# Layer norm's root on four columns, the third modulation product summed by VectorE, and vectors turned first

## What is computed

```python
sc_l = jax.nn.silu(c)
mod_l = (sc_l @ w_mod[i] + b_mod[i])[:, None, :]
sh1_l, s1_l, g1_l, sh2_l, s2_l, g2_l = jnp.split(mod_l, 6, axis=-1)
hl = modulate(rms_norm(xl, norm1_g[i]), sh1_l, s1_l)
...
u = h @ w_pw1 + b_pw1
a, gate = jnp.split(u, 2, axis=-1)
u = a * jax.nn.sigmoid(gate)
u = dwconv(...) + b_dw
u = jax.nn.silu(layer_norm(u, ln_g, ln_b))
yl = u @ w_pw2 + b_pw2
...
xl = xl + g1_l * yl
xl = xl + g2_l * sq_relu_mlp(modulate(rms_norm(xl, norm2_g[i]), sh2_l, s2_l), mlp_w1[i], mlp_w2[i])
```

## Time and profile before

| what | value |
|---|---|
| median of 3 runs | 2220.65 us (2217.94, 2220.65, 2222.88) |
| span of the profiled execution | 2221.3 us, its own time, 0.65 above that median |
| PE busy | 2162.8 us (97%) |
| DVE busy | 989.9 us (45%) |
| ACT busy | 374.7 us (17%) |
| POOL busy | 75.3 us (3%) |
| chain that ended last | PE 66%, issue 23%, DMA 6%, DVE 4%, ACT 1% |
| HBM read | 561.05 MB, 254 GB/s over the span |

### The profile page before, as it was taken

One profiled execution on the slowest core, in us unless ns is written; L12 is line 12 of the kernel. 1 busy time (PEld: TensorE's weight loads), 2 busy tenths in 40 slices (PEclk: granted clock), 3 DMA queues, 4 the chain that ended last, 5 costly groups with the idle time before them and its releaser, 6 DMA issues.

```text
span 2221.3 us, 25048 instructions
## 1 busy us (share of the span) xinstructions
PE 2162.8 (97%) x10192; PEld 1318.6 (59%) x10192; DVE 989.9 (45%) x1433; ACT 374.7 (17%) x743; POOL 75.3 (3%) x94
## 2 busy tenths in 40 slices
PE   7999999999999999998999999999999899999999
PEld 3443588888886777855444444437888544444443
DVE  2983397798845534833112222215555322222222
ACT  3013312012123112842100000002000200000000
POOL 1110100000021000000000000001000000000000
PEclk9999999999999999997999999999999899999999
DMA  9538244677541112032899999996112499999997
GB/s 349 189 95 296 76 152 152 238 259 282 206 171 38 39 52 77 1 152 114 356 429 428 429 428 429 428 424 254 60 76 91 205 422 429 429 428 428 429 428 301
DMA packets 110139, 570.26 MB, mean 257 GB/s; under 512 B 9929, under 2 KB 18670, under 8 KB 82414
## 3 DMA queue, kind: packets, MB, share of 16 engines
q1 hardware_dynamic: 107328, 564.55, 63.3%
q10 hardware_dynamic: 2734, 4.64, 0.9%
HBM read 561.05 MB, written 2.10 MB: 254 GB/s over the span
## 4 chain that ended last, share of the span: by engine, by line
PE 66%; issue 23%; DMA 6%; DVE 4%; ACT 1%; ACTq 0%; POOL 0%; SPq 0%; DVEq 0%; POOLq 0%
PE psum L1677 22%; PE psum L2142 9%; PE psum L1417 6%; PE psum L2126 4%; PE psum L1825 4%; PE psum L1849 3%; DMA ring<-in_moe_w_down_dram 3%; PE psum L2006 2%; PE psum L2234 2%; PE psum L2180 2%; DMA ring<-in_mlp_w_dram 2%; PE psum L1982 2%; PE psum L1957 2%; PE psum L1624 1%; DVE arena L2475 1%
## 5 line engine op out<-in xcount | busy, mean ns | idle before, releaser
L2142 PE MATMUL psum<-ring,arena 128*64 128x512 f32 x2048 | 445.0, 593 | 4.3 <-DMA ring<-in_moe_w_up_dram 4.3
L2142 PEld LDWEIGHTS psum<-ring,arena 128*64 128x64 f32 x2048 | 144.9, 137 | 299.0 <-issue 286.5
L2126 PE MATMUL psum<-ring,arena 128*64 128x512 f32 x768 | 224.5, 594 | 2.0 <-DMA ring<-in_moe_w_down_dram 2.0
L3036 DVE TENSOR_TENSOR arena<-psum,arena 128x512 f32<-128x512 f32 x32 | 33.9, 1059 | 384.9 <-PE psum L2142 384.9
L1417 PE MATMUL psum<-hT,ring 128*128 128x512 f32 x416 | 182.9, 600 | 3.0 <-ACT hT L938 3.0
L1677 PE MATMUL psum<-ring 128*128 128x256 f32 x640 | 142.9, 380 | 2.2 <-DVE roots L2619 2.2
L1417 PEld LDWEIGHTS psum<-hT,ring 128*128 128x128 f32 x416 | 79.6, 192 | 103.6 <-issue 98.6
L1677 PE MATMUL psum<-hT,ring 128*128 128x256 f32 x608 | 139.5, 386 | 0.8 <-ACT hT L932 0.8
L1677 PEld LDWEIGHTS psum<-ring 128*128 128x128 f32 x640 | 121.0, 190 | 22.1 <-issue 5.9
L2180 PEld LDWEIGHTS psum<-arena 128*128 128x128 f32 x1024 | 121.2, 198 | 14.0 <-issue 14.0
L1677 PEld LDWEIGHTS psum<-hT,ring 128*128 128x128 f32 x608 | 117.6, 194 | 18.7 <-issue 2.2
(11 more groups left out here) (417 smaller groups left out, 2535.8 us busy)
## 6 DMA issues: line engine op xcount, KB each, us to landing
ring<-in_moe_w_gate_dram SPq DMA_DIRECT2D x64, 2048.0 KB, 19.1
ring<-in_moe_w_up_dram SPq DMA_DIRECT2D x64, 2048.0 KB, 16.2
ring<-in_moe_w_down_dram SPq DMA_DIRECT2D x44, 2048.0 KB, 19.7
ring<-in_ada_w_dram SPq DMA_DIRECT2D x24, 2048.0 KB, 8.7
ring<-in_mlp_w_dram SPq DMA_DIRECT2D x16, 2048.0 KB, 8.6
hT<-in_moe_w_down_dram SPq DMA_DIRECT2D x16, 2048.0 KB, 14.6
ring<-in_w_mod_dram SPq DMA_DIRECT2D x12, 2048.0 KB, 13.6
ring<-in_conv_w_in_dram SPq DMA_DIRECT2D x6, 2048.0 KB, 19.4
```

The source lines that it names most:

```text
L2126: ins = pe.matmul(psum[64 * e:64 * e + 64, bank + nh, :], src[:, 4 * h + k, 64 * e:64 * e + 64], w[:, k, nh * N:(nh + 1) * N], start=h == ...
L2142: ins = pe.matmul(psum[64 * nh:64 * nh + 64, bank + e, :], src[:, 4 * h + k, 64 * e:64 * e + 64], w[:, k, nh * N:(nh + 1) * N], start=h == ...
```

## The change

**Start.** T_V is turned ahead of `norm_stat(NORM1)`. ACT begins with a one-element SiLU, takes SiLU of c before the root, and so loads its table before the first squares. The first block of `pw1` lands on two semaphores, one for each half.

**Layer norm.** `norm_stat(LN)` becomes eight `token_sums`; the root and reciprocal are taken on 128x4 values; `token_widen(LN)` spreads them into a bank that DVE's `scale` reads directly. A one-element square root goes ahead of the squares.

**Round 2.** `mod_gemv(2)` leaves PE. DVE multiplies and accumulates the four blocks with eight instructions of 2048 columns (`mod_rows_of`), PE sums the result over partitions with four matmuls (`mod_sum(2)`) ahead of tile 5 of `pw2`, and `mod_turn(2)` stands ahead of tile 6. POOL does NORM2's sums before round 2's bias. Weights of the MLP's first two blocks now wait for DVE's reading of round 2.

**Widening.** All widening is done by `pe.transpose` where it was a matmul.

```diff
@@ constants, stream
+MOD_SUMS = {2: (2, 0), 3: (3, 1), ...}
+MOD2_ORDER = (2, 3, 0, 1)
-                    ("mod_row", rnd + 1)) for b in range(4)]
+                    ("mod_part", MOD2_ORDER.index(b) + 1) if rnd == 2 else ("mod_row", rnd + 1)) for b in range(4)]
@@ ACT
             act.wait_ge(S["pads_zero"], 5)
+            act.activation(tok[:, 2, 0:1], one[:, 0:1], ACT.Silu)
             squares(NORM1, xT, emptied(T_X))
-            root(NORM1)
             act.wait_ge(*emptied(T_V)(0))
             act.activation(cpad[:, :, 0:3], ..., ACT.Silu).then_inc(S["c_silu"], 1)
+            root(NORM1)
...
+            act.activation(tok[:, 2, 0:1], one[:, 0:1], ACT.Sqrt)
             squares(LN, cv, lambda j: (S["centered"], j + 1))
-            root(LN)
+            token_root(LN)
             shift(LN, hT, vecT[:, COL["ln_b"]:COL["ln_b"] + 8], ACT.Silu)
-            mod_row(2)
-            mod_turned(2)
...
+                if j == 4:
+                    mod_row(2)
+                if j == 5:
+                    mod_turned(2)
@@ PE
-                    ins = pe.matmul(psum[...], n_tok[:, 1, tt:tt + 1].to_broadcast([P, P]), ident,
-                                    start=True, stop=True, skip_group_check=True)
+                    ins = pe.transpose(psum[...], n_tok[:, 1, tt:tt + 1].to_broadcast([P, P]), ident)
...
-            norm_stat(NORM1)
             pe.wait_ge(S["vec_in"], 16 * N_VEC)
             turn_tile(T_V, ...)
+            norm_stat(NORM1)
...
-            norm_stat(LN)
-            mod_gemv(2)
             for j in range(DT):
-                if j == 1:
+                pe.wait_ge(S["sq_ready"], DT * LN + j + 1)
+                token_sums(sq[:, j % 2, :], j == 0, j == DT - 1).then_inc(S["sq_used"], 1)
+            token_widen(LN)
+            for j in range(DT):
+                if j == 5:
+                    mod_sum(2)
+                if j == 6:
                     mod_turn(2)
@@ DVE
+            def mod_rows_of(b):
+                acc = carve(arena, 10240, 4 * N)
+                w = arrived(dve, B_MOD[2][b])
+                for k in range(2):
+                    c = cpad[:, 2 * b + k, 0:1]
+                    ... ins = tensor_scalar or scalar_tensor_tensor(out=acc, in0=w[:, k, :], scalar=c, in1=acc, ...)
+            for b in MOD2_ORDER[0:2]:
+                mod_rows_of(b)
             for j in range(DT):
+                if j in (1, 2):
+                    mod_rows_of(MOD2_ORDER[j + 1])
                 dve.wait_ge(FREE["act"], tile_free[T_PW2 + j][1])
                 dve.tensor_tensor(xT[:, j, :], xT[:, j, :], tmp[:, j % 2, :], ALU.add).then_inc(S["x_pw2"], 1)
```

More of the change, by code:

```diff
@@ L246, in block_kernel @@
             loads[2] -= PAIRS
-        loads[slot] += len(src) if isinstance(src, list) else 1
+        loads[slot] += len(src) if isinstance(src, list) and n != B_PW1[0] else 1
         landed_at.append((slot, 16 * loads[slot]))
@@ L543, in block_kernel @@
         IN_HALVES = {NORM2: 0, MIX1: 1}
+        INVERSES = {LN: 1, NORM2: 2, MIX1: 3}
         HALF_ORDER = [(j, half) for js, half in ((0, 0), (0, 1), (4, 1), (4, 0)) for j in range(js, js + 4)]
@@ L564, in load @@
                     for m, dst in enumerate(slot_like(slot, src)):
-                        sp.dma_start(dst, src[m]).then_inc(landed[slot], 16)
+                        sp.dma_start(dst, src[m]).then_inc(S["pw1_first"] if (n, m) == (B_PW1[0], 0) else landed[slot], 16)
                 else:
@@ L814, in _ @@
                 .then_inc(S["gains"], 1)
+            sum_squares(NORM2)
+            mod_bias(2)
             make_gain(1, 0, 32, ("norm2_g", 0))
-            sum_squares(NORM2)
             for rnd in range(3, 9):
@@ L918, in token_root @@
             def token_root(n):
-                if n == NORM2:
-                    act.wait_ge(S["sq_used"], DT * NORM2 + DT)
+                if n == MIX1:
+                    act.wait_ge(S["n_ms"], 1)
                 else:
-                    act.wait_ge(S["n_ms"], 1)
+                    act.wait_ge(S["sq_used"], DT * n + DT)
                 act.activation(n_tok[:, 0, :], psum[:, STAT, 0:NT], ACT.Sqrt, bias=eps[:, 0:1])\
@@ L941, in mod_row @@
                 act.wait_ge(S["mod_row"], s + 1)
-                act.activation(mod_rows[:, :], psum[:, MISC, :], ACT.Copy, scale=1.0 if s < 3 else float(P))\
+                act.activation(mod_rows[:, :], psum[:, MISC, :], ACT.Copy, scale=1.0 if s < 2 else float(P))\
                     .then_inc(S["mod_row_sb"], 1)
@@ L1468, in token_widen @@
             def token_widen(n):
-                pe.wait_ge(S["n_inv"], IN_HALVES[n] + 1)
+                pe.wait_ge(S["n_inv"], INVERSES[n])
                 for tt in range(NT):
-                    ins = pe.matmul(psum[:, (MISC, STAT)[tt // 2], tt * P:(tt + 1) * P],
-                                    n_tok[:, 1, tt:tt + 1].to_broadcast([P, P]), ident,
-                                    start=True, stop=True, skip_group_check=True)
-                    if tt % 2:
+                    ins = pe.transpose(psum[:, STAT if n == LN else (MISC, STAT)[tt // 2], tt * P:(tt + 1) * P],
+                                       n_tok[:, 1, tt:tt + 1].to_broadcast([P, P]), ident)
+                    if tt == NT - 1 or tt % 2 and n != LN:
                         ins.then_inc(S["n_wide"], 1)
@@ L1541, in x_widen @@
                 for tt in range(NT):
-                    ins = pe.matmul(psum[:, bank, tt * P:(tt + 1) * P], x_inv[:, which, tt:tt + 1].to_broadcast([P, P]), ident,
-                                    start=True, stop=True, skip_group_check=True)
+                    ins = pe.transpose(psum[:, bank, tt * P:(tt + 1) * P], x_inv[:, which, tt:tt + 1].to_broadcast([P, P]), ident)
                 ins.then_inc(S["x_wide"], 1)
@@ L2369, in scale @@
             def scale(n, src, dst, gains, width=N, made=0):
-                if n:
-                    dve.wait_ge(S["scaled"], DT * SCALES[n])
-                dve.wait_ge(S["rms_ready"], n + 1)
-                link(dve.reciprocal(rstd[:, 0:width], rms[:, 0:width]))
+                if n == LN:
+                    dve.wait_ge(S["n_wide"], 1)
+                    inverse = psum[:, STAT, :]
+                else:
+                    dve.wait_ge(S["rms_ready"], n + 1)
+                    link(dve.reciprocal(rstd[:, 0:width], rms[:, 0:width]))
+                    inverse = rstd[:, 0:width]
                 if made:
@@ L2390, in scale_halves @@
                     j, half = HALF_ORDER[at]
-                    dve.wait_ge(S["n_wide"], 2 * IN_HALVES[n] + half + 1)
+                    dve.wait_ge(S["n_wide"], 2 * IN_HALVES[n] + half + 2)
                     dve.scalar_tensor_tensor(out=hT[:, j, H * half:H * half + H], in0=xT[:, j, H * half:H * half + H],
```

32 lines of the change are left out of this document (22 added, 10 removed).

## The result

| | before | after |
|---|---|---|
| median of 20 runs each, us | 2218.73 | 2223.17 |
| ratio after to before | | 1.0017, 95% interval 1.0011 to 1.0023 |
| span of the profiled execution, us | 2221.3 | 2222.2 |
| PE, DVE, ACT busy, us | 2162.8, 989.9, 374.7 | 2157.0, 1004.9, 373.2 |

By the ratio the change costs 3.8 us (2.4 to 5.1; the medians differ by 4.4), which is inside the 0.2% that was named as the bound of "no change". (One of the 20 executions after took 4566.84 us; the ratio leaves it out.) The forecast was 2223.3 us.

A forecast was written before the change was run, and what follows sets the result against it. PE, busy for 97% of the span, was taken to bound the kernel. Terms -1.4 + 2.8 + 2.2 + 0.9 - 1.8 = +2.7 us on the median 2220.65 gave 2223.3 us; range 2216.0 to 2227.0, the forecast's own 2220.3 to 2226.0.

The forecast's parts named there:

- step 1: Program's start: vectors turned before the norm's sums, SiLU before the root; round 0 begins at 25.0, not 26.41: -1.4 us.
- fourth rival: Program's start: vectors land 2 us later than in the one profile, so no gain there; +4.1, 2224.8 us; 8%.
- Step 2: Layer norm's root: one-column sums mostly at the lower clock, so `pw2` starts at 208.7, not 205.89: +2.8 us.
- first rival: Layer norm: the clock holds through the one-column sums and `pw2` loses nothing; -5.0, 2215.7 us; 12%.
- Step 3: Start of `pw2`: 4.4 us run at half speed because the clock is still low: +2.2 us.
- Step 4: Round 2: PE gets four 512-column matmuls back, DVE's eight added instructions stay hidden: +0.9 us.
- Step 5: Widening by transposes at NORM2, MIX1 and the mixer: four tiles cost 0.9, not 1.7, at the lower clock; -1.8 us.

The follow-up runs named there:

- the start and widenings alone: Kernel before with the vectors turned ahead of the first sums, SiLU of c first, and the four widenings by transposes; 2220.21 us, ratio 0.9998.
- start: Kernel before with only the new order at the program's beginning: SiLU of c ahead of the root, vectors turned ahead of the sums; 2219.00 us, ratio 0.9997.
- widenings: Kernel before with only the four places of widening (NORM2, MIX1, the mixer's two) done by transposes; 2217.04 us, ratio 0.9991.
- interleaved kernel: Kernel before with new opening order, transposed widening, layer norm's root on columns, round 2's product on PE in pieces between one-column sums; 2234.94 us, ratio 1.0061.

## Why the prediction came out

The forecast of 2223.3 met the median of 2223.17, but part of that is luck: the three runs shown of before had a median of 2220.65, the 20 runs one of 2218.73. What was forecast is +2.7, what was measured +3.8 (2.4 to 5.1). The mechanism in the layer norm is the forecast's, the lower clock through sums and the start of `pw2`. But the gain of step 1 is not shown, and the stage before was taken too cheap; these two errors lie in opposite senses. The time alone does not tell the forecast from its fourth rival, *the start gives nothing*, with 2224.8 us and +4.1.

The prediction also compared unlike numbers. It took the profiled execution's span, 2221.3, for its time, 0.65 above the median. Over the runs that list both, the time is some 1.8 us above the span; so that execution took about 2223.1 us (an estimate), some 4.4 more than the median of the 20 runs. It was a slow execution and not a middle one. The sum does not use this, but every term was read from that profile.

**Step 1, the start, -1.4.** Mis-sized, and by more than the profile after shows. There the vectors' transposes began at 17.72 and not 17.3: the step took the ACT queue's last packet, 17.1 to 17.2, as the time PE sees, and PE went on half a us later. The greater error is the base. The delay of the sums was counted from 16.40, the latest of the three old-order starts. Over the profiles they start at 18.2 in the new order and at 15.8 in the old, a delay of 2.5 us and not 1.1. What the new order saves is as much: round 0 starts 7.5 us behind the first sum (9.0 where the clock fell) and not 10.0. With three clock falls in the new sums, round 0 starts at 26.2 on average and not at 25.0, where the old order has 25.8. So the runs show no gain where -1.4 was in the sum. That is the last rival, priced at 8%; its reason, later landings, is half of what the profiles show, and the base is the other half.

**Step 2, +2.8.** Right, a little large. The sums took 12.81 and not 13.4, since the fall came 1.1 us into them and not 0.5 (3.9 us behind the last dense matmul; forecast 3.5, and 2.8 at MIX1); the small steps behind took 3.4, forecast 3.3. The stage costs +2.2. That the clock would fall under a fully busy PE was the point on which forecast and first rival parted, and the earlier trace rows decided it; no profile with these sums showed the rival.

**Step 3, +2.2.** `pw2` ran 5.3 us at half speed and not 4.4: +2.65.

**Step 4, +0.9.** `mod_sum` 1.00 us, DVE 2.37 us a sum (forecast 2.35), no wait.

**Step 5, -1.8.** Four tiles at the lower level cost 0.85 (forecast 0.9), NORM2's first half 0.70 (forecast 0.7). Alone the step measured -2.0 (-4.0 to 0.0).

**The sum.** Steps 2 to 4 were forecast at +5.9. The kernel after against the start and widenings alone measures 1.0017 / 0.9998, +4.2 us (about 2 to 6.6, by both intervals). One cause that the runs show is that the profile before was a lucky one in this stage. Its sums ran at 1.00, but of five profiles with the same dense sums and product (before twice, start, widenings, both) three lost 1.5 to 1.7 us to the clock. On average the change replaces a stage that costs about 0.9 us more than the earlier trace rows show. Steps 1 and 5 were forecast at -3.2 and together measured -0.4 (-2.4 to +1.6). That step 1 gives nothing would account for half or more of the shortfall; `pw1`'s weights for 0.25 us at most, and not in the kernel after. With +0.4 for step 1 in place of -1.4, and 0.9 off for the lucky stage, the sum is 2.7 + 1.8 - 0.9 = +3.6, an estimate from few profiles, beside the +3.8 measured.

**Not foreseen** was how far single profiles mislead about a step of 1 to 3 us here. The spans differ by 0.9 us and the medians by 4.4, because the execution profiled before was 4.4 us slower than its median and the one profiled after (2224.02) only 0.9.

## What to carry to other kernels

Moving a reduction to four one-column matmuls a tile makes the root cheap and the sums dear. Count the records at the lower clock (1.6 to 1.8 us a tile here, against 0.96 for a dense sum), and add what the dense work behind them loses until the clock is back. Before you shorten a path, look at whether PE has dense work in its waits: the kernel with five useless matmuls in two waits, ending before what is waited for, measured -3.6 us here and the one without them -0.4, and such ones between one-column sums cost time. An order that makes PE wait for a landing is priced by the latest landings of several executions, and by the clock behind the wait. Where a change is worth less than the clock's luck, take the stage's times from several profiles before adding terms from one, and compare a profiled execution's span with other spans, not with times.

## What was not expected of the hardware

The clock falls, and stays down, while PE is fully busy with one-column sums: it was down for 20.5 us in both profiles of the kernel after, and for the first 11.7 of them in the first profile PE did nothing but these sums. Alternating dense work did not bring it back in the interleaved kernel: it was at 0.50 for 27 us with 1.9 us dense in every 3.7. The Trainium skill (page "TensorE: Matmul & The Clock Gate", section "Why this matters for your kernels") names long idle gaps of PE between matmuls as what drops the clock. The falls just behind a wait of 2.17 us, in three of six profiles with dense sums, are of that kind; the fall at 197.2 behind waits of at most 0.7 us, and the lower clock under sums that keep PE at a busy share of 1.00, are not covered by it.

By "Part 4: PE-mode transpose" of the same page of the Trainium skill the widenings by transposes should have cost what they gained. Nothing here bears that out: their time fell from 1.71 to 0.85 us a group, and the kernel with them alone is no slower (0.9982 to 1.0000).

It is also new that the same wait of 2.17 us ahead of the same dense sums leads to a fall in some executions and not in others; what in the execution decides it was not found.
